# A decoder layer on one core: the first feed-forward product as seven block products over two token halves

## The reference

```
proj = rmsnorm(h, norm_mix_g) @ w_in
h    = h + concat(gmlp_chunk_mixer(proj[:, :2048]), ssd_mixer(proj[:, 2048:])) @ w_out
hid  = relu(rmsnorm(h, norm_mlp_g) @ w_ff1)          # w_ff1: 1024 x 4096
h    = h + (hid * hid) @ w_ff2                       # w_ff2: 4096 x 1024
gate = sigmoid(rmsnorm(h, ple_norm_g) @ w_ple_gate)
h    = h + gate * (p @ w_ple_proj)
out  = rmsnorm(h, final_norm_g)
```

## Time and profile before

| what | value |
|---|---|
| median of 3 runs | 748.49 us |
| the profiled execution, its own time | 747.09 us |
| its span, first to last instruction | 745.3 us |
| TensorE (PE) busy | 735.0 us, 99% |
| weight loads (PEld), beside PE | 606.4 us, 81% |
| VectorE (DVE) busy | 454.1 us, 61% |
| ScalarE (ACT) busy | 382.9 us, 51% |
| GpSimd (POOL) busy | 107.3 us, 14% |
| moved by transfers | 105.58 MB, mean 142 GB/s |

### The profile page before, as it was taken

How to read it: one execution, slowest core, us unless ns; L and a number is a source line. 1 busy time by engine, 2 the same in 40 slices (tenths; PEclk the granted TensorE clock), 3 DMA queues, 4 the chain that set the end, 5 groups by cost and what they waited for, 6 DMA issues and landing times.

```text
span 745.3 us, 8676 instructions
## 1 busy us (share of the span) xinstructions
PE 735.0 (99%) x3396; PEld 606.4 (81%) x3396; DVE 454.1 (61%) x500; ACT 382.9 (51%) x516; POOL 107.3 (14%) x88
## 2 busy tenths in 40 slices
PE   8999999999999999999999999999999999999996
PEld 7888877788878888888888888888888888888884
DVE  5556794576667465546444952576454942589764
ACT  6524456644674833304564633572266524575775
POOL 1031000766455000000012000020001000200000
PEclk9999999999999999999999999999999999999998
DMA  9732223342241163100976685477727792585311
GB/s 332 210 86 86 87 85 99 124 143 86 93 162 57 57 214 125 58 29 14 373 234 148 140 297 150 84 143 231 227 63 156 192 275 97 118 192 178 106 57 56
DMA packets 47872, 105.58 MB, mean 142 GB/s; under 512 B 4668, under 2 KB 6360, under 8 KB 47832
## 3 DMA queue, kind: packets, MB, share of 16 engines
q1 hardware_dynamic: 40968, 84.03, 33.7%
q0 software_dynamic: 5632, 16.78, 12.4%
q10 hardware_dynamic: 1232, 4.23, 1.6%
HBM read 88.21 MB, written 4.23 MB: 124 GB/s over the span
## 4 chain that ended last, share of the span: by engine, by line
PE 98%; DMA 1%; ACT 0%; issue 0%; DVE 0%; SPq 0%; DVEq 0%
PE acc L1487 28%; PE acc L1489 28%; PE acc L1488 28%; PE side L1549 3%; PE side L1488 2%; PE side L1489 2%; PE side L1487 2%; PE side L1646 2%; PE side L1613 1%; PE side L1653 1%; PE side L1641 1%; DMA gain<-in_norm_mix_g 1%; PE acc L1570 0%; PE side L1593 0%; PE side L1594 0%; PE side L1633 0%
## 5 line engine op out<-in xcount | busy, mean ns | idle before, releaser
L1487 PE MATMUL acc<-w_hi,a_hi 128*128 128x512 f32 x256 | 104.5, 408 | 0.0
L1489 PE MATMUL acc<-w_hi,a_lo 128*128 128x512 f32 x256 | 100.2, 391 | 0.0
L1488 PE MATMUL acc<-w_lo,a_hi 128*128 128x512 f32 x256 | 99.9, 390 | 0.0
L1487 PE MATMUL acc<-b_hi,ring_hi 128*128 128x512 f32 x256 | 99.7, 390 | 0.0
L1489 PE MATMUL acc<-b_hi,ring_lo 128*128 128x512 f32 x256 | 99.7, 389 | 0.0
L1488 PE MATMUL acc<-b_lo,ring_hi 128*128 128x512 f32 x256 | 99.7, 389 | 0.0
L664 ACT ACTIVATE ring_hi<-quarter 128x1024 fp32r<-128x1024 f32 x56 | 56.5, 1051 | 51.3 <-PE acc L1489 34.7
L1293 DVE TENSOR_TENSOR ring_lo<-ring_raw,ring_hi 128x1024 fp32r<-128x1024 f32 x32 | 38.6, 1223 | 67.0 <-ACT ring_hi L664 67.0
L1293 DVE TENSOR_TENSOR ring_lo<-quarter,ring_hi 128x1024 fp32r<-128x1024 f32 x56 | 66.0, 1220 | 17.0 <-ACT ring_hi L664 17.0
L568 POOL DMA_DIRECT2D quarter<-quarter x24 | 20.8, 868 | 351.1 <-DMA quarter<-in_w_ff 223.1
L993 DVE TENSOR_TENSOR w_lo<-w_raw,w_hi 128x1024 fp32r<-128x1024 f32 (+1 forms) x40 | 50.8, 1272 | 27.9 <-ACT w_hi L587 27.4
(11 more groups left out here) (231 smaller groups left out, 1471.8 us busy)
## 6 DMA issues: line engine op xcount, KB each, us to landing
quarter<-in_w_ff SPq DMA_DIRECT2D x40, 512.0 KB, 4.8
w_raw<-in_w_in SPq DMA_DIRECT2D x36, 512.0 KB, 3.7
ring_raw<-in_w_ff SPq DMA_DIRECT2D x32, 512.0 KB, 4.9
quarter<-quarter POOLq DMA_DIRECT2D x24, 512.0 KB, 6.1
w_raw<-in_w_out SPq DMA_DIRECT2D x16, 512.0 KB, 3.4
h<-in_x SPq DMA_DIRECT2D x8, 512.0 KB, 4.3
seg<-cs_dram ACTq DMA_DIRECT2D x8, 512.0 KB, 3.9
quarter<-in_w_ff POOLq DMA_DIRECT2D x8, 512.0 KB, 6.3
```

The lines of the kernel that those rows point to most:

```text
L1487: pe.matmul(dst, st[0], mv[0], start=start, stop=False)
L1488: pe.matmul(dst, st[0], mv[1], start=False, stop=False)
L1489: return pe.matmul(dst, st[1], mv[0], start=False, stop=stop)
```

## The change

The first product is done by the seven-product scheme too. Its left operand is now the transposed tokens in four blocks (token half x feature half), each 512 features x 256 tokens, with four sums S1 to S4 made once by DVE (`x_sum`) and split once (`x_split`). Its right operand is the 1024x1024 block of w_ff1 in four quarters, with T3, T2 and T4 made by adding transfers and T1 by DVE (`make_t1`: T2 minus B22). So both weight matrices now go through the same four quarter buffers, and there are 14 forms per unit where there were 11. A matmul of the first product streams 256 tokens, and there are 7 x 16 x 3 of them per unit where there were 4 x 16 x 3 with 512.

The seven results of the first product are put together to the four hidden blocks C11 to C22: ACT copies two of them out of PSUM (`copy_product`), DVE makes seven combinations (`combine`), and ACT makes relu and square in place on blocks of 128x1024 (`hidden`). The second product's order becomes B11, B21, T3, T2, T1, T4, B22. The gate's transposed tokens get buffers of their own (`g_hi`, `g_lo`), the ple rows a buffer `ple`, and the gate's banks are turned by two. The core of the diff:

```diff
-FORMS = 11
-PRODUCTS = ("B11", "T3", "T2", "T1", "T4", "B21", "B22")
-A_FORMS = ("A11", "S3", "S2", "S1", "A22", "A12", "S4")
+FORMS = 14
+FIRST = ("B11", "B21", "B22", "T2", "T3", "T1", "T4")
+FIRST_A = ("A11", "A12", "S4", "S2", "S3", "S1", "A22")
+SECOND = ("B11", "B21", "T3", "T2", "T1", "T4", "B22")
+SECOND_A = ("A11", "A12", "S3", "S2", "S1", "A22", "S4")
...
+            def load_quarter(u, m, name):
                 i = QUARTER[name]
+                if u or m:
+                    v, q = (u, 0) if m else (u - 1, 1)
+                    user = {0: "T1", 1: "T4", 2: "B21", 3: "B22"}[i]
+                    sp.wait_ge(form_lo, form_count(v, q, user, 1))
+                    if name == "B21":
+                        for p in range(2):
+                            sum_landed(sp, v, q, "T4", p)
+                    if name == "B22" and m:
+                        sp.wait_ge(t1_made, 2 * u + 2)
...
+            for u in range(UNITS):
+                load_quarter(u, 1, "B22")
+                load_quarter(u, 1, "B12")
+                load_quarter(u, 1, "B21")
+                load_quarter(u, 1, "B11")
                 reload_b12(u)
+                if u < UNITS - 1:
+                    load_quarter(u + 1, 0, "B21")
+                    load_quarter(u + 1, 0, "B12")
+                    load_quarter(u + 1, 0, "B11")
+                    load_quarter(u + 1, 0, "B22")
...
             for u in range(UNITS):
-                for name in SUMS:
-                    for p in range(2):
-                        t_add(u, name, p)
+                for m in range(2):
+                    for name in ("T3", "T2", "T1", "T4") if m else ("T3", "T2", "T4"):
+                        for p in range(2):
+                            t_add(u, m, name, p)
...
+            def make_t1(u, p):
+                at = (slice(None), slice(2 * p, 2 * p + 2))
+                sum_landed(dve, u, 0, "T2", p)
+                dve.wait_ge(form_lo, form_count(u, 0, "T3", p))
+                dve.tensor_tensor(quarter[0][at], quarter[1][at], quarter[3][at], ALU.subtract).then_inc(t1_made, 1)
+
+            def combine(u, what):
+                dst, left, right, op = {
+                    "C11": ("A11", "A21", pair(1), ALU.add), "U": ("A21", pair(1), "A21", ALU.subtract),
+                    "C12 part": ("A12", "A12", "A21", ALU.add), "U3": ("A21", "A21", pair(0), ALU.add),
+                    "C12": ("A12", "A12", pair(1), ALU.add), "C22": ("A22", "A21", pair(1), ALU.add),
+                    "C21": ("A21", pair(0), "A21", ALU.subtract)}[what]
```

DVE's order in one unit (what only unit 0 has, the x forms among it, is left out):

```diff
+                both(2)
...
+                both(3)
...
+                combine(u, "C11")
+                both(4)
+                for p in range(2):
+                    make_t1(u, p)
+                both(5)
+                split_a(u, "A11")
+                combine(u, "U")
+                combine(u, "C12 part")
+                both(6)
+                combine(u, "U3")
...
+                both(7)
+                combine(u, "C12")
+                combine(u, "C22")
+                both(8)
+                combine(u, "C21")
+                split_a(u, "A12")
+                both(9)
+                s_add(u, "S3")
+                s_add(u, "S1")
+                split_a(u, "S3")
+                s_add(u, "S2")
+                s_add(u, "S4")
+                both(10)
+                split_a(u, "S2")
+                h_add(u, "B21")
+                split_a(u, "S1")
+                both(11)
+                h_add(u, "T3 right")
+                h_add(u, "T3 above")
+                both(12)
+                split_a(u, "A22")
+                h_add(u, "T2")
+                both(13)
+                split_a(u, "S4")
+                if last:
+                    for what in LAST_ADDS:
+                        h_finish(what)
+                else:
+                    both(14)
                 h_add(u, "T4")
```

ACT's order behind `both(8)`, and TensorE's first product:

```diff
+                hidden(u, "A12")
+                split_a(u, "A12")
+                both(9)
+                hidden(u, "A21")
+                hidden(u, "A22")
+                split_a(u, "S3")
...
+            def product_f1(u, j):
...
+                if j < 2:
+                    pe.wait_ge(*((h_added, add_count(u - 1, ("T4", "B22")[j])) if u else emptied(PLE, 2 + j)))
+                elif j in (2, 4):
+                    pe.wait_ge(p_copied, 2 * u + j // 2)
+                else:
+                    pe.wait_ge(combined, combined_count(u, {3: "C11", 5: "U", 6: "U3"}[j]))
                 for i in range(4):
                     for k in range(4):
                         if i == 0 and k % 2 == 0:
                             pe.wait_ge(form_lo, 2 * n + k // 2 + 1)
+                        ins = product(pair(j % 2)[:, i, :], [t[:, k, i * P:i * P + P] for t in (hi, lo)],
+                                      [t[name][:, k, :] for t in (x_hi, x_lo)], k == 0, k == 3)
```

More of the change, by code:

```diff
@@ L72, in build_layer @@
             gain = sb("gain", [P, 2, D], where=early)
-        def form(name, tiles, width):
-            hi = sb(name + "_hi", [P, tiles, width], F32R)
-            with ExitStack() as first:
-                raw = sb(name + "_raw", [P, tiles, width], where=first)
-            lo = sb(name + "_lo", [P, tiles, width], F32R)
-            return hi, raw, lo
-        quarter = [sb(f"quarter{i}", [P, 4, 512]) for i in range(2)]
-        ring = {0: form("ring0", 4, 512)}
-        ring[2] = form("ring2", 4, 512)
@@ new lines, in raw_lo, with raw_hi @@
+        def raw_lo(name):
+            with ExitStack() as first:
+                raw = sb(name + "_raw", [P, 4, 256], where=first)
+            return raw, sb(name + "_lo", [P, 4, 256], F32R)
+        def raw_hi(name):
+            with ExitStack() as first:
+                raw = sb(name + "_raw", [P, 4, 256], where=first)
+            return raw, sb(name + "_hi", [P, 4, 256], F32R)
+        quarter = [sb(f"quarter{i}", [P, 4, 512]) for i in range(2)]
+        ring = {0: split_pair("ring0", 4, 512)}
@@ new lines, in build_layer @@
+        ring[2] = split_pair("ring2", 4, 512)
+        ring[1] = split_pair("ring1", 4, 512)
+        quarter += [sb(f"quarter{i}", [P, 4, 512]) for i in range(2, 4)]
+        with ExitStack() as early:
+            g_hi = sb("g_hi", [P, KT, SEQ], F32R, where=early)
+            g_lo = sb("g_lo", [P, KT, SEQ], F32R, where=early)
+        x_hi, x_lo, x_raw = {}, {}, {}
+        for name in ("A11", "A12"):
+            x_hi[name], x_lo[name] = split_pair("x" + name, 4, 256)
+        x_raw["A11"], x_hi["S2"] = raw_hi("xA11_S2")
@@ L329, in add_count, with combined_count, hid_count, s_count @@
             return 2 + len(ADDS) * u + ADDS.index(what) + 1
-        LO_COUNT = {"A11": 1, "S3": 2, "S2": 3, "S1": 4, "A22": 6, "A12": 6, "S4": 7}
+        COMBINED = ("C11", "U", "C12 part", "U3", "C12", "C22", "C21")
+        def combined_count(u, what):
+            return 7 * u + COMBINED.index(what) + 1
+        HID = ("A11", "A12", "A21", "A22")
+        SUMS = ("S3", "S1", "S2", "S4")
+        HI_ORDER = ("A11", "A12", "S3", "S2", "S1", "S4", "A22")
+        LO_ORDER = ("A11", "A12", "S3", "S2", "S1", "A22", "S4")
+        X_SUMS = ("S1", "S2", "S4", "S3")
+        X_ORDER = ("S4", "S2", "S3", "S1", "A22")
+        def hid_count(u, name):
+            return 4 * u + HID.index(name) + 1
+        def s_count(u, name):
+            return 4 * u + SUMS.index(name) + 1
+        def hi_count(u, name):
+            return 7 * u + HI_ORDER.index(name) + 1
+        def lo_count(u, name):
+            return 7 * u + LO_ORDER.index(name) + 1
         block = ctx.enter_context(nc.Block())
@@ new lines, in split_form @@
+                if name[0] == "B":
+                    act.wait_ge(q_landed[i][p], quarter_count(u, m, name))
+                elif name == "T1" and m == 0:
+                    act.wait_ge(t1_made, 2 * u + p + 1)
+                else:
+                    sum_landed(act, u, m, name, p)
+                if n >= 3:
+                    act.wait_ge(ff_step, 2 * (n - 2))
+                else:
+                    act.wait_ge(acc_full, 4 * (OUT + 4) if n < 2 else 4 * (PLE + 1))
+                act.activation(ring[n % 3][0][at], quarter[i][at], ACT.Copy).then_inc(form_hi, 1)
@@ new lines, in product_f1, with product_f2 @@
+                    if i % 2:
+                        ins.then_inc(ff_step, 1)
+            def product_f2(u, j, between=None):
+                n = FORMS * u + 7 + j
+                hi, lo = ring[n % 3]
+                name = SECOND[j]
+                left = [t[SECOND_A[j]] for t in (f_hi, f_lo)]
+                bank = {"B11": side[:, 0:2], "T1": side[:, 2:4], "B21": acc[:, 2:4], "T3": acc[:, 0:2],
+                        "T2": acc[:, 2:4], "T4": acc[:, 0:2], "B22": acc[:, 2:4]}[name]
+                if u == UNITS - 1 and name == "B22":
@@ L1739, in product_f2 @@
+                if name == "B21":
+                    pe.wait_ge(combined, combined_count(u, "C22"))
+                elif name == "T3":
```

(6 more changed lines are left out.)

601 lines of the change are left out of this document (288 added, 313 removed).

## The result

The changed kernel takes **791.1 us** (median of 4 runs, 787.45 to 792.67) against 748.49 on the same chip: ratio 1.0567, 95% interval 1.0528 to 1.0606. The prediction said 763 and a range of 741 to 780. The sign was right; the loss is 42.6 us where some 15 were foreseen, and the time lies outside the range.

What follows compares the result with a forecast made beforehand. TensorE, 98% of the chain, was taken as the bound: -12.8 for shorter records, +10.5, 4, 4 and 8 for waits in four units, +1.3 behind them, +15.0; on the median 748.5 + 14.5, rounded 763 us, range 741 to 780.

Steps and rivals of the forecast that it cites:

- part 4: Chain of one unit: late forms and engine order make TensorE wait 10.5, 4, 4 and 8 us in units 0 to 3.
- the landings of T4's second half and of B11's loads: Between first and second product: T4's second half lands after about 7 us, B11's loads after 7.6 and about 8.5.
- the granted clock behind a wait: TensorE's clock may drop briefly after waits of more than some 3 us: bound 0 to 3 us, taken 0.
- Part 1: First product's matmuls: 1344 records of 256 columns at 0.120 us replace 768 at 0.2267, saving 12.8 us.
- Rival C: First product: each narrow record costs a whole weight load of 188 ns, +79, 827 us; chance 0.03.
- Part 2: Other engines per unit: DVE 62 us, ACT about 45, neither filling 78.4; no cost in themselves, though order can cost.
- Part 3: Transfers per unit: adding ones rise from 8 to 14, load from 51.4 to 68.7 us, fitting into 78 but unevenly.
- A12, S3, h11: Second product: waits for A12's remainder 1.4, S3 0.9 and the add to h11 1.4 us, together 3.7 per unit.
- The sum on the median: Whole kernel: +15.0 on the profiled 747.1, written as 748.5 + 14.5 on the median, rounded to 763 us.
- rival A: Transfers are hidden, B11 lands before 37 and waits shrink: 744 us, or 735 with records at 109 ns; chance 0.22.
- B: Rival: queues saturate, meetings of transfers cost some 7% more, 2 to 3 us per unit: +28, 776 us; chance 0.15.
- ACT's waits for transfers pass 5 us per unit: Sign in each unit that the saturated-queue rival holds and the prediction fails.

Runs made afterwards that it cites:

- e11: e8 with DVE's C12, C21 and B21's sum into h done on a sixteenth of their columns, the rest left out: 773.6 us, ratio 1.0354.
- e8: e5 with a second DVE order (C21, S1's difference and B21's sum into h moved earlier): 774.1 us, ratio 1.0347.
- e3: Changed kernel with only SP's load order for the second product altered to B21, B11, B22, B12: 775.6 us, ratio 1.0375.
- e1: Changed kernel with the first product's T4 summed on DVE instead of by adding transfers: 773.5 us, ratio 1.0355.
- e10: e8 with the first product's T3 and T2 summed by DVE on 16 of 512 columns, without their 4 adding transfers: 770.8 us, ratio 1.0310.
- e13: e8 with the second product's adding transfers for T2 and T1 on 32 of 512 columns, the rest unsummed: 753.1 us, ratio 1.0063.
- e14: e13 together with e11's cut of DVE work: 751.1 us, ratio 1.0051.
- e5: e3 with S3's work ahead of T3's form on ACT and DVE, and the first product's T4 on DVE: 772.0 us, ratio 1.0334.
- e7: Changed kernel with only S3's work moved first in the engine order, transfers as they were: 809.7 us, ratio 1.0842.

## Why the prediction was right and wrong

- **The steps that failed** are two terms of the sum, both in part 4 and both mis-sized: the landings of T4's second half and of B11's loads, and the granted clock behind a wait. The first made waits at B11 of 15.9 us in units 1 to 3, where none was taken; the second cost about 14 us over the stage, where 0 was taken. That is about the 30.4 us missed; the smaller terms below nearly cancel.
- **Part 1, the narrow records: right.** 0.120 us measured, 0.120 taken, so -12.8 us is there. The Trainium skill's formula for a single gap ("TensorE: Matmul & The Clock Gate", section "Back-to-back issue gap") gives 109 ns for this record; the trace says 120, so it does not agree. The first halves of units 1 to 3 run without a wait of 0.3 us and more, except 1.0 in unit 2. Rival C, the whole weight load of 188 ns, is refuted by the same rows.
- **Part 2: right in kind.** No engine is full as such: taking 3.2 us per unit from DVE (e11) changed 0.5 us.
- **Part 3, that 68.7 us of transfers "fit into 78, but not evenly": right and not followed up.** The unevenness was the case. In e8 what is in series lies in some 35 us at a DMA share of 0.86, behind 28.6 us at 0.50.
- **Part 4, the chain of one unit: every link right, two landings mis-sized.** "It lands after about 7 us" (T4): 11.3. "7.6 and about 8.5" (B11): 11.0 and 11.9. That is 4.3 and 3.4 us more. T4's also went out 1.5 us late, and there were 1.7 us of slack in front of T4's form and 1.8 behind B11's first one (the 0.3 in the prediction is against its second half), so 5.6 us of wait are left at B11 in unit 1. I took the rows of a pair that meets one or two loads, where four loads and two adding transfers meet now. e3 shows the term by itself: without the meeting T4's second half takes 6.1 us and B11's second load 6.8.
- **The clock, "bound 0 to 3 us, taken 0": mis-sized, its bound too.** 2.9 us are lost behind unit 1's wait alone, and about 14 in the whole stage, where the granted clock averages 0.95. The bound is about right for one wait, but the term stood in the sum for the whole kernel. It also comes behind shorter waits than the 3 us named: behind the 2.5 us for P1's copy 1.6 are lost here (and 0.2 behind the same wait in e1).
- **A12, S3, h11 (1.4 + 0.9 + 1.4 per unit):** in unit 1 the first two vanished in B11's longer wait; the third is a wait of 1.2 with 0.2 behind it, 1.4 as taken. Unit 3: 17.9 for 8; unit 0: 16.6 for 10.5. There P1's copy was waited for 2.5 us (2.1 taken), B11 4.2 as taken, and 1.8 us before the first half's T4, which the prediction does not have and which are gone in e1 and e3.
- **The sum on the median:** 748.5 + 15.0 would be 763.5; the 14.5 in its place changes nothing.
- **What the prediction's frame missed:** it stopped its chain at the add to h11. The second product's own series (T3, T2, reload, T1) now starts after T4's form. It did not show in the changed kernel's waits: T1's form was there 3.4 us before TensorE came to it. Once the waits in front of it were shortened (e8 to e11), it held TensorE at 84 to 86 us per unit, and no cure of the landings or of the order tried here came near rival A's 78.4 plus a little.
- **The rivals.** A asked for B11 landing before 37; it landed at 44.8 on that clock (505.7 - 460.9), so it fell. B, with 776 us, was the nearest in mechanism and still 15 short: I let a meeting cost 7% more, and it cost 40 to 60%. Its sign "ACT's waits for transfers pass 5 us per unit" is far exceeded: 12.3 us for B11's first load alone in unit 1. The range failed since its upper end lay near B's, worked out with the same small surcharge and without the clock.

## What to carry to other kernels

When a change makes buffers serve a second use in the same unit, write down the whole series of transfers from the moment the buffer comes free to the last form that needs it, with every engine's form in it, and compare its length with the time until TensorE wants it; the share averaged over the unit (0.69 to 0.76 here) hides a stretch at 0.86. Price a landing by how many transfers will be in flight, not by the nearest row with one. Price each new wait of TensorE with what the clock may take behind it. And when several cures each bring the same part of a loss and then stop at the same pitch, look for the next bound by shortening one suspect at a time with little columns, as e10, e11 and e13 did, before building more order.

No version here beats the kernel before: even with the series and DVE's work cut (e14) it stays at 1.0051. In e13 12.8 us of shorter records stand against some 18 us that are left: 12.4 of waits and the rest behind them, at each unit's T2 (6), in unit 0 (4) and at the end (8).

## What the runs showed of the hardware

- A 512 KB adding transfer between quarters lands after 4.6 us alone and 6.1 as second of a pair (e3, unit 1), and after 11.3 with four loads beside it (changed kernel, unit 1). T4's two, issued right behind T1's, took 9.5 and 11.4 in e8.
- In the changed kernel 512 KB loads that met two adding transfers took 11.0 and 11.9 us; the same two without them, but with other loads beside, 5.2 and 6.8 (e3).
- The lower clock behind a wait is no fixed price. Behind 5.58 us 2.9 were lost, behind 3.2 us (e5, unit 1) 1.7, behind 3.2 us in the next unit of the same run nothing over 0.25; behind 1.84 us (e1, unit 2) 1.7. What decides was not tried and stays open.
- A wait can cost more than its own length: from the changed kernel's profile to e7's (spans 790.9 and 807.1 us) the waits grow by 7.5 us and the loss at the lower clock by some 10.
